# A decoder layer's opening: small tables on ScalarE's DMA queue, another buffer for the spatial weights, and the first x tiles in one row

## The reference, cut to what matters

```python
mod = silu(c) @ w_ada + b_ada                 # (1 + 8) rows x 6*1024: shift, scale, gate, twice
h = x * (1 + sc1) + sh1
proj = h @ w_in                               # 2048 columns, split among three mixer groups
y_a = b * conv3(c * x)                        # 256 channels, conv_w, state_conv
y_b = u * (tril(w_s) @ layer_norm(v) + b_s)   # 8 heads x 64, one 128x128 matrix w_s per head
y_c = (window means - z) @ pool_w * pool_scale  # windows 2, 4, 8, 16, state_pool
x = layer_norm(alpha * x + g1 * (concat(y_a, y_b, y_c) @ w_out))
h2 = x * (1 + sc2) + sh2
x = layer_norm(alpha * x + g2 * (relu(h2 @ w_up) ** 2 @ w_down))
```

## Time and profile before

| what | us |
|---|---|
| median of 3 runs | 2292.63 (2291.53 to 2293.13) |
| the profiled execution | 2290.67 |
| its span in the trace | 2288.9 |
| PE busy | 2200.6 |
| first matmul with a weight slab | 37.23 from the start of the span |

### The profile page before, as it was taken

The page is one execution under the profiler, slowest core; times in us unless marked ns, Lnnn a source line. Parts: engine busy times, 40 slices in busy tenths (PEclk is TensorE's granted clock), DMA queues, the critical chain, the costliest instruction groups (busy, mean ns, idle before and its releaser), DMA issues.

```text
span 2288.9 us, 27030 instructions
## 1 busy us (share of the span) xinstructions
PE 2200.6 (96%) x10746; PEld 1812.3 (79%) x10746; DVE 1314.9 (57%) x1927; ACT 628.9 (27%) x872; POOL 982.7 (43%) x427
## 2 busy tenths in 40 slices
PE   7989999999989999999999999999999999999993
PEld 4556887878888888888888888888888888888882
DVE  1555568686585734654476654376664475555337
ACT  1201323223212332333223234232333322222221
POOL 3312333433322343544645444564544464444335
PEclk9999999999999999999999999999999999999997
DMA  8545453343332244433234343333433322333221
GB/s 255 173 129 168 138 166 111 96 171 102 116 126 88 83 146 145 132 101 113 82 110 144 118 122 111 95 92 120 149 114 115 97 83 93 116 102 95 84 66 42
DMA packets 262832, 269.37 MB, mean 118 GB/s; under 512 B 13080, under 2 KB 220137, under 8 KB 262706
## 3 DMA queue, kind: packets, MB, share of 16 engines
q1 hardware_dynamic: 262706, 267.64, 37.4%
HBM read 249.78 MB, written 17.81 MB: 117 GB/s over the span
## 4 chain that ended last, share of the span: by engine, by line
PE 66%; DVE 3%; POOL 2%; issue 0%; DMA 0%; ACT 0%; DVEq 0%
PE ps L827 22%; PE ps L829 22%; PE ps L828 22%; POOL acc L691 1%; PE ps L960 1%; POOL w_hilo L667 0%; DVE htmp L1381 0%; DMA w_raw<-in_w_up 0%; DVE xt L1631 0%; DVE xt L1554 0%; DVE st L1183 0%; DVE spl L1204 0%; DVE acc L1375 0%; DVE hid L1540 0%; POOL xt L697 0%
## 5 line engine op out<-in xcount | busy, mean ns | idle before, releaser
L667 POOL TENSOR_TENSOR w_hilo<-w_raw,w_hilo 128x1024 fp32r<-128x1024 f32 x352 | 907.3, 2586 | 1275.2 <-ACT w_hilo L726 1275.1
L726 ACT ACTIVATE w_hilo<-w_raw 128x1024 fp32r<-128x1024 f32 x352 | 365.3, 1054 | 1077.3 <-PE ps L829 1021.4
L1588 DVE TENSOR_TENSOR acc<-acc,ps 128x512 f32<-128x512 f32 (+1 forms) x510 | 344.5, 686 | 234.2 <-PE ps L829 231.0
L827 PE MATMUL ps<-w_hilo,hid 128*128 128x512 f32 (+1 forms) x1088 | 424.1, 390 | 1.5 <-DVE acc L1585 1.1
L828 PE MATMUL ps<-w_hilo,hid 128*128 128x512 f32 (+1 forms) x1088 | 423.8, 389 | 0.0
L829 PE MATMUL ps<-w_hilo,hid 128*128 128x512 f32 (+1 forms) x1088 | 423.4, 389 | 0.0
L827 PE MATMUL ps<-hA,w_hilo 128*128 128x512 f32 (+1 forms) x992 | 373.5, 376 | 8.3 <-DVE acc L1410 4.2
L829 PE MATMUL ps<-hA,w_hilo 128*128 128x512 f32 (+1 forms) x992 | 371.3, 374 | 0.0
L828 PE MATMUL ps<-hA,w_hilo 128*128 128x512 f32 (+1 forms) x992 | 371.1, 374 | 0.0
L1540 DVE CAST hid<-htmp 128x512 fp32r<-128x512 f32 (+1 forms) x128 | 59.6, 465 | 391.7 <-ACT htmp L772 391.0
L827 PE MATMUL ps<-hB,w_hilo 128*128 128x288 f32 (+1 forms) x768 | 250.7, 326 | 0.0
(11 more groups left out here) (185 smaller groups left out, 2387.2 us busy)
## 6 DMA issues: line engine op xcount, KB each, us to landing
w_raw<-in_w_up SPq DMA_DIRECT2D x128, 512.0 KB, 4.1
w_raw<-in_w_down SPq DMA_DIRECT2D x128, 512.0 KB, 3.6
w_raw<-in_w_in SPq DMA_DIRECT2D x64, 512.0 KB, 4.0
xt<-in_w_ada SPq DMA_DIRECT2D x22, 1024.0 KB
w_raw<-in_w_out SPq DMA_DIRECT2D x32, 512.0 KB, 3.7
xt<-in_x_prompt SPq DMA_DIRECT2D x16, 512.0 KB, 6.4
x_norm<-xt SPq DMA_DIRECT2D x16, 512.0 KB, 6.3
xt<-x_norm SPq DMA_DIRECT2D x16, 512.0 KB, 6.0
```

What stands on the lines that cost most here:

```text
L667: pool.tensor_tensor(W[:, g % SLOTS, 1, :], raw[:, g % RAW, :], W[:, g % SLOTS, 0, :], ALU.subtract).then_inc(lo_done, 1)
L726: act.activation(W[:, g % SLOTS, 0, :], raw[:, g % RAW, :], ACT.Copy).then_inc(hi_done, 1)
L827: pe.matmul(out, w_hi, x_hi, start=start, stop=False)
L1588: dve.tensor_tensor(a, a, src, ALU.add).then_inc(d_evac, 1)
```

## The change

- The twelve small loads are issued by ACT, ahead of its `Silu`. After the `Silu` ACT waits for `s_prep` and issues the four loads of `pool_w`, waits for `s_pret` and issues the eight corner copies, and only then goes on to `x0_affine`.
- `w_s` is loaded into `raw[:, 1]`, the second buffer of the weight slabs, in place of `g1row`.
- SP issues piece 0, 1 and 2 and x tiles 0, 1, 2 and 3 in one row, with a wait for `s_cT` (the turned `c`) ahead of tile 3. Slab 0 follows, ahead of piece 3. Slab 1 comes behind piece 4 and a wait for `s_pret`.

```diff
-        prep, w_s_rows, c_rows = acc[:, 2:4, :], g1row, xs[:, 0, :]
+        prep, w_s_rows, c_rows = acc[:, 2:4, :], raw[:, 1, :], xs[:, 0, :]
...
             ada_weights(0)
             ada_bias_in(0)
-            sp.dma_start(w_s_rows[:, :].rearrange("p (h j) -> p h j", h=HEADS),
-                         w_s[0].rearrange("h i j -> i h j")).then_inc(s_pre, 16)
...
-            sp.dma_start(xt[0:ST, 4, :], x_sample.rearrange("b t d -> (b t) d")).then_inc(s_pre, 16)
             for u in range(1, 3):
                 ada_weights(u)
                 ada_bias_in(u)
             x0_load(0)
             x0_load(1)
-
-            sp.wait_ge(s_prep, 1)
-            for g in range(4):
...
-            sp.wait_ge(s_pret, 1)
-            for b in range(NB):
...
             x0_load(2)
+            sp.wait_ge(s_cT, 1)
             x0_load(3)
...
+            slab(0, free=False)
             ada_weights(3)
             ada_bias_in(3)
-            for n in range(RAW):
-                slab(n, free=False)
             ada_rows_out(0)
             ada_piece(4)
+
+            sp.wait_ge(s_pret, 1)
+            slab(1, free=False)
...
         def _(act):
+            act.dma_start(w_s_rows[:, :].rearrange("p (h j) -> p h j", h=HEADS),
+                         w_s[0].rearrange("h i j -> i h j")).then_inc(s_pre, 16)
...
+            act.dma_start(xt[0:ST, 4, :], x_sample.rearrange("b t d -> (b t) d")).then_inc(s_pre, 16)
             act.wait_ge(s_cT, 1)
             act.activation(siluT[:, :], ps[:, 0, 0:KD * (1 + NB)], ACT.Silu).then_inc(s_silu, 1)
+
+            act.wait_ge(s_prep, 1)
+            for g in range(4):
+                q, c = 64 * (g % 2), g // 2
+                act.dma_start(prep[q:q + 64, 0, P * c + q:P * c + q + 64], pool_w[0, g]).then_inc(s_corner, 16)
+            act.wait_ge(s_pret, 1)
+            for b in range(NB):
+                act.dma_start(prep[DT * b:DT * b + DT, 0, 2 * P:2 * P + HEADS * ST].rearrange(
...
+                             ).then_inc(s_corner, 16)
```

More of the change, by code:

```diff
@@ L448, in _ @@
             x0_load(1)
-            sp.wait_ge(s_prep, 1)
-            for g in range(4):
-                q, c = 64 * (g % 2), g // 2
-                sp.dma_start(prep[q:q + 64, 0, P * c + q:P * c + q + 64], pool_w[0, g]).then_inc(s_corner, 16)
-            sp.wait_ge(s_pret, 1)
-            for b in range(NB):
[L456 to L459, removed]
             x0_load(2)
+            sp.wait_ge(s_cT, 1)
             x0_load(3)
@@ L716, in _ @@
         def _(act):
+            act.dma_start(w_s_rows[:, :].rearrange("p (h j) -> p h j", h=HEADS),
+                         w_s[0].rearrange("h i j -> i h j")).then_inc(s_pre, 16)
+            act.dma_start(htmp[0:NB * CONV_BUF, 0, 0:W_CONV],
+                         state_conv[0].rearrange("b r c -> (b r) c")).then_inc(s_pre, 16)
+            act.dma_start(htmp[0:NB * POOL_BUF, 1, 0:W_POOL],
+                         state_pool[0].rearrange("b r c -> (b r) c")).then_inc(s_pre, 16)
+            for half in range(2):
+                act.dma_start(gate_tab[64 * half:64 * half + 64, :, :],
+                             bcast(b_s[0].rearrange("(q two) i -> two q i", two=2)[half], 64)
+                             ).then_inc(s_pre, 16)
+            for c in range(2):
+                act.dma_start(convw[:, c, :],
+                             conv_w[0, :, P * c:P * c + P].rearrange("w p -> p w")).then_inc(s_pre, 16)
+            act.dma_start(pscale[:, :], pool_scale[0].rearrange("(c p) -> p c", p=P)).then_inc(s_pre, 16)
+            act.dma_start(sgu_gT[:, :], sgu_g[0].rearrange("(c p) -> p c", p=P)).then_inc(s_pre, 16)
+            act.dma_start(lnT[:, 0, :], ln1_g[0].rearrange("(k p) -> p k", p=P)).then_inc(s_pre, 16)
+            act.dma_start(lnT[:, 1, :], ln1_b[0].rearrange("(k p) -> p k", p=P)).then_inc(s_pre, 16)
+            act.dma_start(xt[0:ST, 4, :], x_sample.rearrange("b t d -> (b t) d")).then_inc(s_pre, 16)
             act.wait_ge(s_cT, 1)
             act.activation(siluT[:, :], ps[:, 0, 0:KD * (1 + NB)], ACT.Silu).then_inc(s_silu, 1)
+            act.wait_ge(s_prep, 1)
[5 more added lines that the diff above has]
+                act.dma_start(prep[DT * b:DT * b + DT, 0, 2 * P:2 * P + HEADS * ST].rearrange(
+                                 "p (h i) -> p h i", h=HEADS)[:, :, DT * b:DT * b + DT],
+                             prep[0:DT, 1, :].rearrange("p (h i) -> p h i", h=HEADS)[:, :, 0:DT]
+                             ).then_inc(s_corner, 16)
             def hi_part(g, free=True):
```

## The result

| what | us |
|---|---|
| after, median of 8 runs | 2296.78 (2292.96 to 2301.54) |
| before, median of 8 runs on the same chip | 2292.88 (2289.02 to 2294.72) |
| ratio after to before | 1.0025 [1.0015, 1.0034] |
| profiled execution of after | 2292.96, span 2290.9 |
| first matmul with a weight slab | 43.33, before 37.23 |

The ratio makes it 5.7 us slower (2292.88 x 0.0025), with an interval of 3.4 to 7.8 us. The two medians are only 3.9 us apart, because five of the eight runs of after lie from 2293.0 to 2297.3 and three from 2300.9 to 2301.5. The profiled execution is the lowest of the eight.

What follows compares the result with a forecast made beforehand. PE's schedule was taken to bound the kernel, through the start of `v_slab(0, 0)`. Late tables (25.7 us) plus the chain gave 4.2 us, and 1.3 was added: 5.5 on 2292.63 made 2298.1, range 2288.2 to 2303.2.

Steps and rivals of the forecast that it cites:

- The whole moves with `v_slab(0, 0)`: Opening: everything behind the first slab matmul, at 37.23 us before, shifts by as much as that start does.
- The bound of 4.2 us for a gain: Opening: DMA work ahead of product 3 lets `v_slab(0, 0)` start no sooner than 33.0 us, a gain of 4.2.
- Two queues alternate packet by packet, so the tables come last: Opening loads: SP's and ACT's queues take turns by packets, so the small loads finish arriving at 25.7 us.
- A: Rival, opening: the tables arrive early, by 16 us, and the DMA bound rules; 4.2 us less, chance 0.22.
- B: Rival, opening: tables land near 21.5 us, the DMA hole of 2.1 us is won and lost on PE; no change, chance 0.11.
- The chain from the tables on: Opening: PE's serial work from the `w_s` transposes to `v_slab(0, 0)` takes 15.65 us, POOL deciding its last part.
- ACT is held: Opening: a full queue holds ACT's issues until 17 to 18 us, so product 0 ends at 23 to 25, just ahead of the tables.
- C: Rival, opening: ACT isn't held, piece 3 shares with the tables and product 1 runs at 1.2 GHz; +10.3 us, chance 0.27.
- The sum: Whole kernel: 4.2 us for the later start plus 1.3 for a small share of piece 3 slipping in, 5.5 us slower.
- Corner copies on ACT have cover: Opening: ACT's corner copies take 6.0 us and finish 1.1 us before the affines are due.
- The DMA hole closes and x tiles no longer make PE wait: Opening: the DMA hole at 22.5 to 25.5 us goes, 2.1 us of full DMA work at most; PE never waits for x tiles.
- Behind the start every row keeps its place: After the first slab matmul: every profile row stands where it stood relative to that start.

Runs made afterwards that it cites:

- e7: The changed kernel with its seven loads of single floats read as runs of 8 to 32 bytes, 896 packets for 3,584: 2291.97 us, ratio 1.0004 to before.
- e9: The changed kernel with `w_s` and both states loaded by SP behind piece 0, the nine other small loads by ACT behind `hi_part(2)`: 2290.38 us, 0.999 to before.
- e10: e9 with slab 0 issued behind piece 3 instead of ahead of it: 2287.79 us, ratio 0.9989 to before.
- e3: The kernel before with only the twelve small loads moved to ACT ahead of its `Silu`: 2304.4 us, ratio 1.0057 to before.
- e1: The changed kernel with the `Silu` ahead of the twelve small loads on ACT: 2303.95 us, ratio 1.0053 to before.
- e8: The kernel before with only the nine later-used small loads moved to ACT behind `hi_part(1)`: 2287.55 us, ratio 0.9982 to before.
- e2: The changed kernel with the twelve small loads back on SP behind piece 0, the rest of the change kept: 2291.17 us, ratio 0.9997 to before.
- e4: The changed kernel with the seven loads of single floats behind the `Silu`, five loads (1,736 packets) ahead of it: 2302.97 us, ratio 1.0046 to before.

## Why the prediction was right

Predicted were 2298.1 us, 5.5 more than before, by the mechanism that was likeliest; measured are 2296.8 by the median and 5.7 more by the ratio.

- **The whole moves with `v_slab(0, 0)`: right** while the move is a delay. The start is 6.1 us later and the whole 5.7 slower. It isn't so for an earlier start: e7, e9 and e10 lose most of it again a dozen microseconds later. The bound of 4.2 us for a gain would have been worth less than it says, since it stops at the first slab matmul.
- **Two queues alternate packet by packet, so the tables come last: right.** 1,241 packets against 1,240. I had the tables at 25.7, and they landed at 26.6. A and B fall with that, and e7 shows the cause by itself.
- **The chain from the tables on: right.** 15.65 us worked out, 15.61 measured, with POOL still ending the last wait (1.24).
- **ACT is held, and C doesn't come to pass: right, but the hold was mis-sized**, and this is the term that failed. I let ACT pass its last issue at 17 to 18, when some 3,300 packets were through. The queue drained a little faster than I had it: the trace counts 2,879 of ACT's packets by 14.4 and 3,305 by 15.9. But the queue holds less than the 2,000 I assumed. The twelve loads put 5,320 + 12 x 16 = 5,512 records in the queue (16 more for each load, as e3 shows, where the twelve loads were all that ACT issued: 5,511), so 5,512 - 3,882 = 1,630 were left when the issue ended. Without its own 80 that is 1,550; the three held issues ahead of it ended with 1,637, 1,786 and 1,658 records of earlier loads left, counted in the same way, and those in e1 with 1,275 to 1,703. The issue of `pool_scale` with 1,480 ahead of it wasn't held (0.51). On top came the table load of 1.28, which I had placed at the head. The `Silu` ran at 22.11, and product 0 ended at 27.7 instead of 23 to 25, 1.1 us behind the tables.
- **The sum.** I had 4.2 for the chain and 1.3 as a share of C, 5.5. Measured: 4.1 for the chain (25.7 + 15.65 - 37.23), 0.9 for tables that landed later and 1.1 for product 0 that ended behind them, 6.1. The share of C had no part in it: piece 3 was issued at 27.82, when the tables had landed. So 1.3 for something that didn't happen stood in for 2.0 of two things that I had left out, and that 5.5 and 6.1 lie so close is in part luck. C's own mechanism is real where ACT isn't held: e1 starts 10.6 us late, and I had 10.3.
- **Corner copies on ACT have cover: right**, 5.98 us from 31.20, over 0.75 us ahead of the affine at 37.93; I had 1.1.
- **The DMA hole closes and x tiles no longer make PE wait: right, and no gain by itself.** With the tables last, it only keeps the loss small: without these parts the move would cost 11.8 us and not 6.1 (e3).
- **Behind the start every row keeps its place: only up to the mixers.** To the transposes of `x_sample` it holds (+6.11). Behind them I had left out that DVE and POOL hold each other up, and that a few hundredths of a microsecond decide which waits: that, with the clock behind it, takes most of the delay back in the profiled execution. In the MLP before takes 1449.2 us from first to last `relu`, after 1449.3.
- **What the profile after would show.** I had PE waiting for a DMA at the `w_s` transposes until 24 to 28. They started at 27.72 but behind product 0, so the wait shown is the `Silu`'s. e1 shows the other.

## What to carry to other kernels

Where two queues have work, count their packets, not their bytes: single floats in one queue each take a turn from the weights in the other, and the weights from them. Don't put a long row of issues ahead of an instruction that the critical path needs; an issue was held here until the packets of the loads ahead of it had come down to some 1,300 to 1,800, and everything behind it on the engine stood with it. Before moving loads to another queue, ask which of them are needed early at all: taking nine late tables out of the opening gave 1.6 us at the first slab matmul and 4 over the whole (e8), where the change lost 6.

## What was unexpected of the hardware

- ACT's DMA issue stood for 6.87 us, and was let go with 1,630 packets outstanding, its own 80 among them; SP's bias issues stood for 6.94 (e1) and 6.22 (e2). With 1,736 packets issued in all (e4) nothing held the `Silu`.
- A DVE operation on two SBUF tensors took 2.71 us instead of 0.69 when it started behind a POOL operation (e2). In e10 a cast took 2.45 for 0.43 as well. It turned 7.9 us gained into 1.5. In the last mixer a start 0.04 us behind POOL's made 2.92 us of 0.76.
